# Six staging buffers, four rows of the expert sum moved to TensorE, and L2 norms by a product with ones, a logarithm and an exponential

## The reference

```python
def l2norm(x):
    return x * lax.rsqrt(jnp.sum(x * x, axis=-1, keepdims=True) + EPS)
...
n = rmsnorm(x, ln1_g)
proj = n @ w_in
qkv, z, lx, ly, ga, gb, bt, dc = split_cols(proj, IN_SPLITS)
qkv_c, dn_buf = causal_conv(qkv, dn_buf0, dn_conv_w)
qkv_c = jax.nn.silu(qkv_c).astype(f32)
q, k, v = jnp.split(qkv_c, [DN_QK, 2 * DN_QK], axis=-1)
q = l2norm(q.reshape(B, T, DN_HEADS, DN_DK)) * (DN_DK ** -0.5)
k = l2norm(k.reshape(B, T, DN_HEADS, DN_DK))
```

## Time and profile before

| What | Value |
|---|---|
| Three runs, median (lowest to highest) | 2141.03 us (2140.2 to 2142.7) |
| Profiled execution: time, span, mean granted clock | 2148.23 us, 2146.4 us, 0.952 |
| PE, PEld busy | 1877.8 us (87%), 1222.9 us (57%) |
| DVE, ACT, POOL busy | 1489.8 us (69%), 853.6 us (40%), 641.1 us (30%) |
| DMA moved | 724.62 MB, mean 338 GB/s |
| ACT_TABLE_LOAD of L1202 (Sqrt), L1207 (Exp of the deltas) | 10 and 9, 1283 ns each |

### The profile page before, as it was taken

One profiled execution on the slowest core, in us unless ns is written; L12 is line 12 of the kernel. 1 busy time (PEld: TensorE's weight loads), 2 busy tenths in 40 slices (PEclk: granted clock), 3 DMA queues, 4 the chain that ended last, 5 costly groups with the idle time before them and its releaser, 6 DMA issues.

```text
span 2146.4 us, 23913 instructions
## 1 busy us (share of the span) xinstructions
PE 1877.8 (87%) x7974; PEld 1222.9 (57%) x7974; DVE 1489.8 (69%) x3280; ACT 853.6 (40%) x2349; POOL 641.1 (30%) x549
## 2 busy tenths in 40 slices
PE   8999999899987899998799678899998877777776
PEld 7888998656655567776566345664454423322321
DVE  4063631388878678789887677888878667667664
ACT  2533111253523476457534135345523333333332
POOL 0000000124422433323334232344434444444432
PEclk9899999899999999999899889999998999999999
DMA  6243234799999999999789999899999999999997
GB/s 228 93 152 128 98 99 169 288 339 356 377 417 399 415 380 387 398 376 368 287 290 362 419 417 352 323 360 393 387 414 418 421 402 421 421 421 422 422 382 302
DMA packets 128564, 724.62 MB, mean 338 GB/s; under 512 B 16384, under 2 KB 23168, under 8 KB 58304
## 3 DMA queue, kind: packets, MB, share of 16 engines
q0 software_dynamic: 78336, 570.46, 66.7%
q1 hardware_dynamic: 49488, 150.49, 19.1%
q10 hardware_dynamic: 624, 2.23, 0.3%
HBM read 714.08 MB, written 8.52 MB: 337 GB/s over the span
## 4 chain that ended last, share of the span: by engine, by line
PE 54%; DMA 23%; DVE 14%; ACT 6%; issue 2%; POOL 1%; DVEq 0%; SPq 0%; POOLq 0%; ACTq 0%
DMA arena<-in_uv,arena 16%; PE ps L1061 13%; PE ps L1009 12%; PE ps L731 6%; DVE arena L1931 6%; PE ps L787 5%; PE ps L927 4%; DMA arena<-in_stream 3%; PE ps L878 2%; PE ps L951 2%; PE ps L868 2%; PE ps L877 2%; DMA arena<-in_w_a 2%; DMA arena<-in_w_out 2%; ACT arena L1456 1%
## 5 line engine op out<-in xcount | busy, mean ns | idle before, releaser
L1495 POOL DMA_INDIRECT arena<-in_uv,arena x544 | 640.0, 1176 | 1201.8 <-PE ps L1061 764.2
L1061 PE MATMUL ps<-arena 128*128 128x512 f32 (+1 forms) x1624 | 787.5, 622 | 119.5 <-ACT arena L1456 119.3
L1931 DVE CUSTOM_DVE_ANT_0 arena<-arena 128x1024 f32<-128x1024 f32 x544 | 659.9, 1220 | 260.4 <-DMA arena<-in_uv,arena 258.4
L1061 PEld LDWEIGHTS ps<-arena 128*128 128x128 f32 (+1 forms) x1624 | 288.4, 191 | 484.6 <-issue 283.1
L1470 ACT ACTIVATE gelu_d<-dots 128x2 f32<-128x2 f32 x272 | 55.4, 204 | 812.4 <-DVE dots L1931 811.6
L1009 PE MATMUL ps<-arena 128*128 128x294 f32 (+1 forms) x1152 | 292.8, 415 | 17.5 <-DMA arena<-in_stream 9.4
L1009 PEld LDWEIGHTS ps<-arena 128*128 128x128 f32 x1152 | 220.4, 192 | 91.4 <-issue 13.5
L927 PEld LDWEIGHTS ps<-arena 128*128 128x128 f32 x1024 | 134.7, 204 | 35.8 <-issue 14.3
L927 PE MATMUL ps<-arena 128*128 128x128 f32 (+1 forms) x1024 | 138.5, 296 | 17.8 <-DMA arena<-in_w_a 13.3
L731 PE MATMUL ps<-arena 128*128 128x256 f32 x640 | 144.1, 389 | 3.5 <-DVE arena L1518 3.0
L731 PEld LDWEIGHTS ps<-arena 128*128 128x128 f32 x640 | 124.8, 196 | 22.1 <-issue 3.4
(11 more groups left out here) (277 smaller groups left out, 2047.2 us busy)
## 6 DMA issues: line engine op xcount, KB each, us to landing
arena<-in_stream SPq DMA_DIRECT2D x144, 512.0 KB
arena<-in_w_a SPq DMA_DIRECT2D x32, 512.0 KB
arena<-in_w_out SPq DMA_DIRECT2D x32, 512.0 KB
arena<-in_w_q SPq DMA_DIRECT2D x32, 512.0 KB
arena<-in_uv,arena POOLq DMA_INDIRECT x544
spill<-arena SPq DMA_DIRECT2D x48, 80.0 KB
arena<-spill SPq DMA_DIRECT2D x2, 1920.0 KB, 15.5
arena<-in_x_t SPq DMA_DIRECT2D x8, 272.0 KB, 4.8
```

The source lines that it names most:

```text
L1061: mm = pe.matmul(ps[0:L, half, :], diag[on_pe(k) % NDIAG][:, 0:L], ring[k % SLOTS][:, D + half * 512:D + (half + 1) * 512], start=False, s ...
L1495: pool.indirect_dma_start(out=ring[kk % SLOTS], out_offset=None, in_=a["uv"], in_offset=bass.IndirectOffsetOnAxis(ap=idx[:, kk:kk + 1], ax ...
L1931: ins = dve.tensor_tensor_reduce(ring[s][:, 0:D], ring[s][:, 0:D], n2p if t == NTILE else n2[t % 2], 1.0, 0.0, ALU.mult, ALU.add, dots[k / ...
```

## The change

1. **x_t in five DMAs.** The eight chunks of the input come in parts of 1, 1, 2, 2 and 2 chunks; ACT's squares wait for the part.
2. **Six staging buffers.** `stg` has six buffers where it had three; ACT's SiLUs, the gates and DVE's products wait for the spill of six places before.
3. **Rows at the end of the projections.** `on_dve` no longer takes the rows of stages BG + 82 to BG + 86: rows 156 to 159 are summed on PE.
4. **The norms.** PE makes one product per group of `ones` (128 by 128) with the squares of q, at b + 1, and one with those of k, at b + 4 behind `d_exp`; each leaves the sums already spread over all partitions, 512 columns. ACT at b + 5 takes Ln of both out of PSUM and one Exp with scale -0.5 over both, in SBUF. Sqrt, reciprocal, `rqk` and the spreading products go, and DVE multiplies out of SBUF once `d_rcp` (now ACT's) is there.

```diff
-            for c in range(KC):
-                sp.dma_start(x_t[:, c, :], a["x_t"][:, c, :]).then_inc(x_in[c], 16)
+            for j, (lo, hi) in enumerate(X_PARTS):
+                sp.dma_start(x_t[:, lo:hi, :], a["x_t"][:, lo:hi, :]).then_inc(x_in[j], 16)
...
+        NSTG = 6
         stg = [view(o3 + 4 * N2 + s * (P + TS), P + TS) for s in range(3)]
+        stg += [sb(f"stg{s}", [P, P + TS])[:, :] for s in range(3, NSTG)]
...
             if BG + LX <= s < BG + 87:
-                return True
+                return s < BG + 82
...
                 yield b + 1
                 pe.wait_ge(d_sq, nth(t, g))
-                for j, src in enumerate((sq_q, sq_k)):
-                    for i in range(HG):
-                        c = j * HG + i
-                        mm = pe.matmul(ps[0:L, 2 + 3 * g + PC, c:c + 1], src[:, hs.start + i, 0:L], ones[:, 0:1],
-                                       start=True, stop=True)
-                mm.then_inc(d_ssq, 1)
+                pe.matmul(bank(PC, P)[:, :, 0:L], ones[:, :], sq_q[:, hs, 0:L], start=True, stop=True).then_inc(d_ssq, 1)

                 yield b + 4
-                pe.wait_ge(d_rcp, nth(t, g))
-                for i in range(HG):
-                    pe.matmul(bank(PC, P)[:, i, 0:L], rqk[0:L, g, i:i + 1].broadcast_to([L, P]), ident[0:L, 0:L],
-                              start=True, stop=True)
                 pe.wait_ge(d_exp, nth(t, g))
-                for i in range(HG):
-                    mm = pe.matmul(bank(PA, P)[:, i, 0:L], rqk[0:L, g, HG + i:HG + i + 1].broadcast_to([L, P]),
-                                   ident[0:L, 0:L], start=True, stop=True)
-                mm.then_inc(d_rbc, 1)
+                pe.matmul(bank(PA, P)[:, :, 0:L], ones[:, :], sq_k[:, hs, 0:L], start=True, stop=True).then_inc(d_rbc, 1)
...
-                yield b + 2
-                act.wait_ge(d_ssq, nth(t, g))
-                act.activation(rqk[0:L, g, :], ps[0:L, 2 + 3 * g + PC, 0:2 * HG], ACT.Sqrt, bias=eps_col[0:L, 0:1]
-                               ).then_inc(d_root, 1)
-
                 yield b + 3
                 act.wait_ge(d_rel, nth(t, g))
                 act.activation(dec[0:L, hs, 0:L], dec[0:L, hs, 0:L], ACT.Exp, scale=-1.0)
                 act.activation(gam[:, hs, 0:L], bank(PA, P)[:, :, 0:L], ACT.Exp).then_inc(d_exp, 1)
+
+                yield b + 5
+                act.wait_ge(d_ssq, nth(t, g))
+                act.activation(sq_q[:, hs, 0:L], bank(PC, P)[:, :, 0:L], ACT.Ln, bias=eps_col[:, 0:1])
+                act.wait_ge(d_rbc, nth(t, g))
+                act.activation(sq_k[:, hs, 0:L], bank(PA, P)[:, :, 0:L], ACT.Ln, bias=eps_col[:, 0:1]
+                               ).then_inc(d_root, 1)
+                act.wait_ge(d_root, nth(t, g))
+                both = view(4 * D, 2, H, P)[:, :, hs, 0:L]
+                act.activation(both, both, ACT.Exp, scale=-0.5).then_inc(d_rcp, 1)
...
                     act.wait_ge(conv_ready, CONVS + KC + m + 1)
-                    act.wait_ge(stg_out[q % 3], uses(q // 3))
+                    act.wait_ge(stg_out[q % NSTG], uses(q // NSTG))
...
-                yield b + 3
-                dve.wait_ge(d_root, nth(t, g))
-                dve.reciprocal(rqk[0:L, g, :], rqk[0:L, g, :]).then_inc(d_rcp, 1)
-
...
                 yield b + 5
-                dve.wait_ge(d_rbc, nth(t, g))
+                dve.wait_ge(d_rcp, nth(t, g))
                 dve.scalar_tensor_tensor(out=q[:, hs, :], in0=q[:, hs, :], scalar=float(P) ** -0.5,
-                                         in1=bank(PC, P)[:, :, 0:L], op0=ALU.mult, op1=ALU.mult)
-                dve.tensor_tensor(k[:, hs, :], k[:, hs, :], bank(PA, P)[:, :, 0:L], ALU.mult).then_inc(d_norm, 1)
+                                         in1=sq_q[:, hs, 0:L], op0=ALU.mult, op1=ALU.mult)
+                dve.tensor_tensor(k[:, hs, :], k[:, hs, :], sq_k[:, hs, 0:L], ALU.mult).then_inc(d_norm, 1)
```

More of the change, by code:

```diff
@@ L206, in trunk_program @@
         params_in = sem("params_in")
-        x_in = [sem(f"x_in{c}") for c in range(KC)]
+        X_PARTS = ((0, 1), (1, 2), (2, 4), (4, 6), (6, 8))
+        x_in = [sem(f"x_in{c}") for c in range(len(X_PARTS))]
         ones_ready = sem("ones_ready")
@@ L300, in trunk_program @@
         g_bb = sem("g_bb")
-        stg_out = [sem(f"stg_out{s}") for s in range(3)]
+        stg_out = [sem(f"stg_out{s}") for s in range(NSTG)]
         qkv_in = sem("qkv_in")
@@ L663, in loads @@
                 sp.wait_ge(d_og, nth(2, 1))
-                for s in range(3):
-                    sp.wait_ge(stg_out[s], uses(2 * KC))
+                for s in range(NSTG):
+                    sp.wait_ge(stg_out[s], uses(6 * KC // NSTG))
                 sp.dma_start(td[3][:, 3 * KC:6 * KC, :], a["spill3"][:, 3 * KC:6 * KC, :]).then_inc(qkv_in, 16)
@@ L676, in put @@
             def put(q, row):
-                sp.dma_start(a["spill3"][:, row, :], stg[q % 3]).then_inc(stg_out[q % 3], 16)
+                sp.dma_start(a["spill3"][:, row, :], stg[q % NSTG]).then_inc(stg_out[q % NSTG], 16)
             def spills():
@@ L1092, in _ @@
             for c in range(KC):
-                act.wait_ge(x_in[c], 16)
+                act.wait_ge(x_in[(c + 2) // 2 if c else 0], 16)
                 act.activation(sq_x[:, c, :], x_t[:, c, :], ACT.Square).then_inc(sq_done, 1)
@@ L1330, in through @@
                     act.wait_ge(tw_used, group_done(c))
-                    if q >= 3:
-                        act.wait_ge(stg_out[q % 3], uses(q // 3))
+                    if q >= NSTG:
+                        act.wait_ge(stg_out[q % NSTG], uses(q // NSTG))
                     x = ps[:, group_bank(p), :]
                     act.activation(td[2][:, j * KC + n, :], x[:, HIST:HIST + P], func)
-                    act.activation(stg[q % 3][:, 0:P], x[:, HIST + P:HIST + N1], func)
-                    act.activation(stg[q % 3][:, P:P + TS], x[:, SMP0:NP2], func).then_inc(g_evac, 1)
+                    act.activation(stg[q % NSTG][:, 0:P], x[:, HIST + P:HIST + N1], func)
+                    act.activation(stg[q % NSTG][:, P:P + TS], x[:, SMP0:NP2], func).then_inc(g_evac, 1)
                 for n in range(KC):
@@ L1372, in silu @@
                     act.wait_ge(conv_ready, CONVS + KC + m + 1)
-                    act.wait_ge(stg_out[q % 3], uses(q // 3))
+                    act.wait_ge(stg_out[q % NSTG], uses(q // NSTG))
                     y = yc[m % 3]
                     act.activation(td[2][:, q, :], y[:, 0:P], ACT.Silu)
-                    act.activation(stg[q % 3][:, 0:P], y[:, P:N1], ACT.Silu)
-                    act.activation(stg[q % 3][:, P:P + TS], y[:, YS0:YS0 + TS], ACT.Silu).then_inc(conv_used, 1)
+                    act.activation(stg[q % NSTG][:, 0:P], y[:, P:N1], ACT.Silu)
+                    act.activation(stg[q % NSTG][:, P:P + TS], y[:, YS0:YS0 + TS], ACT.Silu).then_inc(conv_used, 1)
                 for m in range(3 * KC + 2):
@@ L1667, in delta @@
                 if t == 2:
-                    for s in range(3):
-                        dve.wait_ge(stg_out[s], uses(2 * KC))
+                    for s in range(NSTG):
+                        dve.wait_ge(stg_out[s], uses(6 * KC // NSTG))
                 dve.tensor_tensor(kend[0:L, hs, :], bank(PC), dec[0:L, hs, L - 1:L].broadcast_to([L, HG, P]), ALU.mult
@@ L1814, in second_sums @@
                     dve.wait_ge(g_evac, 3 * KC + n + 1)
-                    dve.wait_ge(stg_out[q % 3], uses(q // 3))
+                    dve.wait_ge(stg_out[q % NSTG], uses(q // NSTG))
                     x, gate_b = ps[:, group_bank(6 * KC + 2 * n + 1), :], sg[n % 2]
                     dve.tensor_tensor(td[2][:, KC + n, :], x[:, 0:P], gate_b[:, 0:P], ALU.mult)
-                    dve.tensor_tensor(stg[q % 3], x[:, P:N2], gate_b[:, P:N2], ALU.mult).then_inc(g_bb, 1)
+                    dve.tensor_tensor(stg[q % NSTG], x[:, P:N2], gate_b[:, P:N2], ALU.mult).then_inc(g_bb, 1)
                 for m in range(3 * KC):
```

1 line of the change is left out of this document (removed).

## The result

The changed kernel takes 1.0071 times the time of the kernel before (95% interval 1.0053 to 1.0089), about 15 us more: four runs between 2152.82 and 2158.88 us against five between 2139.62 and 2142.70. (A fifth run, at a granted clock of 0.623, stands outside the comparison.) The forecast was 2147 with a range of 2132 to 2157, slower. Sign and mechanism came out; the size is more than twice the 6.5 us of the sum. On the median of 2141.03 it is 2156: within the range by 1 us, outside the 2142 to 2152 that the forecast gave itself, and nearest to rival 2 (2154, 2157 at most).

The account below looks back on a forecast made before the run. No single bound: PE in delta 0, elsewhere ACT and DVE chains, waits or DMA. Terms -3.2 + 4.3 - 1.1 + 4.1 + 2.4 = +6.5 us on the 2141.03 median gave 2147 us, range 2132 to 2157.

Parts of the forecast that it names:

- the sum: Whole kernel: the terms for the five deltas, -3.2 + 4.3 - 1.1 + 4.1 + 2.4, make +6.5 us.
- rival 2: Norms' waits cost more than their length through PE's lower clock, and the sample pays 7.2 in full: 2154 us; chance 0.15.
- End of the projections and delta 2: Staging and rows bring delta 2's squares 7.5 us earlier, new norms take back 6.4: -1.1 us.
- the walk: Deltas 1 to 3: ACT's and DVE's new order stepped through with trace durations, giving norm times and +4.3, +6.4, +4.1 us.
- Delta 3: DVE's norm of group 1 comes at 1324.7 against 1320.64, behind ACT's longer norms: +4.1 us.
- Delta 0: PE is the bound and saves 3.5 us per delta, less up to 0.5 of a new ACT wait: -3.2 us.
- Delta 1: ACT starts 1.46 us earlier but its norms grow; DVE's norm of group 1 at about 453.1 against 448.79: +4.3 us.
- Sample: Sample's delta: DVE's norm of group 1 comes 7.2 us late, against some 4 us PE saves; a third taken, +2.4 us.
- x_t: Input in five DMAs, ahead of PE's first projection product: cost nothing, half a microsecond either way as bound.
- rival 1: Deltas' norms: transfers hide the delays, gathers going on meanwhile; faster, 2133 us with 85% hidden; chance 0.28.
- Rival 3: Staging ahead of delta 2: last spills may hold the delta's later waits, so 4.9 of 7.5 us stays away: 2152; chance 0.09.
- Rival 4: ACT's norms: Ln and Exp share a table, saving up to 2.6 us of loads per group: about 2135; chance 0.02.

Follow-up runs that it names:

- e3: The kernel before with the new norms in all five deltas and nothing else changed: 2164.72 us, 1.0115 times the kernel before.
- e2: The changed kernel with the new norms in delta 0 alone, norms of before elsewhere: 2132.56 us, 0.9961 times the kernel before.
- e1: The changed kernel with the norms of before in all five deltas, other three parts kept: 2136.19 us, 0.9987 times the kernel before.
- e10: Second run of the changed kernel with the new norms in delta 0 alone: 2131.10 us, 0.9948 times the kernel before.
- e4: The changed kernel with the norms of before in the sample's delta alone: 2148.68 us, 1.0045 times the kernel before.
- e5: The changed kernel with norms of before and the four rows back on DVE; six staging buffers and five x_t DMAs stay: 2139.42 us, 0.9993.
- e9: The changed kernel with new norms in delta 0; elsewhere narrow products with Ln and Exp over narrow columns, no DVE reciprocal: 2131.95 us, 0.9955.

## Why the prediction was right, point by point, and short in size

- **Sign.** The norms' place on ACT's chain outweighs what PE saves, except in delta 0. e3 and e2 show the two halves apart. The measured 2156 at the very end of the range is part luck: rival 2's "at most" that set this end counted 1.7 us for each of three deltas, and by its own 3.4 it would have been 2162.
- **End of the projections and delta 2**: -7.5 and +6.4 predicted, net -1.1. The squares came 7.9 us earlier, the norms at 1032.37 and 1041.87, which with 3.9 us is 1036.3 and 1045.8: the walk had 1036.4 and 1045.85. Net -1.3 at row 168. The walk was right; the two terms were each 2.5 us too small, and that they cancel is luck: by e1 it is -10.1 and +8.8. The term left out is PE's clock. The walk set the new norms against the old ones as before's trace has them, with PE at a granted clock of 0.79 from 1010 to 1050; with the four rows in PE's idle time the old norms are 2.6 us shorter too (18.43 against 21.00 us, e1), so putting the new ones in their place costs more than the walk's 6.4.
- **Delta 3**: with the 7.6 us by which after is ahead at row 244, the norms stand at 1319.65 and 1324.8; the walk had 1319.5 and 1324.7. Of 4.2 us lost by row 248, 2.9 came back by row 264, which the sum didn't have.
- **Delta 0**: -3.2 predicted, -3.3 measured on PE's stretch (at e2 and e10), -4.2 to -6.7 with tail 0 (row 7 less the shift of PE's first product of delta 0; e10 and e2).
- **Delta 1**: +4.3 predicted, 7.0 measured. The step that failed is the head start, "since the first Sqrt step is gone". It wasn't there to be had: in after the GELU ahead of the Exp waits for a dot, which stands on DVE behind a selection step and another dot that waited for a gathered row, in ACT's and in DVE's timeline:

```profile
424.23 0.20 ACT L1465 ACTIVATE gelu_d<-dots 128x2 f32<-128x2 f32 x1 [2.07 <-DVE dots L1922]
...
425.69 1.28 ACT L1192 ACT_TABLE_LOAD   x1
```

```profile
419.31 1.23 DVE L1922 CUSTOM_DVE_ANT_0 arena<-arena 128x1024 f32<-128x1024 f32 x1 [1.72 <-DMA arena<-in_uv,arena]
```

  From that load to DVE's norm of group 0 it took 11.35 us (425.69 to 437.04), and the walk had 11.2: the chain was right, its start wrong. Deltas 0 and 1 together came to +1.2 in after (row 13, less the 6.3 us of the clock), against the +1.1 of the sum: tail 0's gain makes up for what delta 1 lost more.
- **Sample**: the walk gave 7.2 late, and I took "a third" because rows 1 and 8 named PE and DMA as bounds. It paid 7.8 in full. This is the largest error of the sum, 5.4 us. That PE was busy 43.91 of 45 us did not protect it: PE's next products wait for the norm, and after was busy 35.93 of the same 45 us.
- **Behind the sample**: 4.9 us by row 328 were in no term. e4 shows that they aren't the sample's norms, e5 that the clock moves this stretch by some 9 us in single executions, and all eight kernels of the table lose 2.3 to 10.8 us there against the one trace of before. What of them belongs to the change stays open.
- **x_t**: PE's first product came at 17.54 against 17.67; nothing, as said. It frees the three semaphores that the buffers take.
- **Rivals.** The transfers hid little of the norms (rival 1): the lost time of delta 1 and the sample was there although DMA had been at 0.98 and 0.99, and by e4 and e2 the rows' 19.6 us at deltas 1 to 3 are 18 us of time. Rival 2 came nearest to the time: the sample paid in full, as it said, and its mechanism, PE at its lower clock after new waits, is in the sample's rows above; what that clock alone adds isn't separated by any run. Rival 3 fell: no DVE wait for a spill in delta 2. Rival 4 fell: after has a load ahead of each Ln of q (L1197) and each norm's Exp (L1203), ten of each. (Its sum was off too: 16 us under 2147 is 2131, not 2135.)

## What to carry to other kernels

When a step moves from one engine to another, walk the receiving engine's written order with the durations of the trace, per place, and take the walk's answer in full: here its ends fit within 0.2 us at four norms of deltas 2 and 3, and the one place where it was discounted by judgment was the one most wrong. The same edit can win where the giver is the bound (delta 0) and lose where the receiver is the chain: choose it per place, which gave the fastest kernels here (e2, e10, and e9 with its narrow norms in the other four deltas). Where a chain on ACT grows, look first at what else stands in it: moving its step ahead of a GELU and the other group's Exps took back half of the loss without removing anything.

## What the runs showed of the hardware that I had not expected

- DVE's reciprocal takes 6.4 ns for a column in fp32 (6548 ns for 1024), ACT's Exp over the same columns 1057 ns.
- Activations out of PSUM with a bias column took 688 ns for 512 columns (Ln), where the Exp without one took 578 (the 0.58 us of L1208 in the earlier trace rows); whether function or bias makes the difference isn't shown.
- The granted clock of the first 66 us differs between executions from 0.84 to 0.95 with the same work, worth 6 us here; and in the stretch into tail 3 (1490 to 1570) it was 0.83 in e5 and 0.94 in before, worth some 9. In e5 it fell behind 20 us in which PE had been busy 20.00.
